# Attention heads of a two-layer trunk: one value product per head with features on partitions, probabilities scaled before they are turned, turned two blocks behind, and a rotation of one operation

## What is computed

```python
q = (_rms_norm(cq, g_q) @ w_uq).reshape(b, s, MLA_HEADS, QK_NOPE + QK_ROPE)      # 8 heads, 64 + 32
kv = (_rms_norm(ckv, g_kv) @ w_ukv).reshape(b, s, MLA_HEADS, QK_NOPE + V_DIM)    # 64 + 64
q_pe = _rope(q_pe, cos[:, :, None], sin[:, :, None])
k_pe = _rope(k_pe, cos, sin)
for i in range(s // Q_BLOCK):                                                     # 4 blocks of 128 queries
    scores = (q_nope . k_nope + q_pe . k_pe) * ATTN_SCALE, causal, over (i + 1) * 128 keys
    probs = jax.nn.softmax(scores, axis=-1)
    outs.append(jnp.einsum('bhqk,bkhd->bqhd', probs, v[:, :k_end]))
y = jnp.concatenate([pool_mixer, spatial_gating, attention], axis=-1)
return y @ w_out
```

## Time and profile before

| | us |
|---|---|
| median of 3 runs (2265.99 to 2271.66) | 2271.29 |
| the profiled execution | 2274.56 |
| its span | 2272.8 |
| mean granted PE clock over the span (share of full) | 0.898 |
| PE busy | 1938.4 (85%) |
| DVE busy | 1248.5 (55%) |
| ACT busy | 913.2 (40%) |

### The profile page before, as it was taken

The page is one execution under the profiler, slowest core; times in us unless marked ns, Lnnn a source line. Parts: engine busy times, 40 slices in busy tenths (PEclk is TensorE's granted clock), DMA queues, the critical chain, the costliest instruction groups (busy, mean ns, idle before and its releaser), DMA issues. The chain is left out here.

```text
span 2272.8 us, 31364 instructions
## 1 busy us (share of the span) xinstructions
PE 1938.4 (85%) x8992; PEld 1339.1 (59%) x8993; DVE 1248.5 (55%) x1918; ACT 913.2 (40%) x1339; POOL 364.6 (16%) x281
## 2 busy tenths in 40 slices
PE   6888889889999998999378888988899999999960
PEld 3655577666666665665165456757666666666640
DVE  2457636546464554643754774557464555546437
ACT  2323421435453544543132442146454545444531
POOL 0100300112221211211020030012122221111210
PEclk9888889989998999999689888999899999999985
DMA  6135224589999999998733622457799999999956
GB/s 247 68 126 185 74 105 167 212 334 389 399 376 374 352 385 333 385 374 327 287 102 99 207 79 78 192 187 293 301 400 399 361 373 371 380 363 375 352 220 272
DMA packets 128818, 619.42 MB, mean 273 GB/s; under 512 B 22530, under 2 KB 25602, under 8 KB 73490
## 3 DMA queue, kind: packets, MB, share of 16 engines
q1 hardware_dynamic: 105876, 550.62, 63.5%
q0 software_dynamic: 22784, 67.13, 8.3%
HBM read 584.13 MB, written 46.14 MB: 277 GB/s over the span
## 5 line engine op out<-in xcount | busy, mean ns | idle before, releaser
L1564 DVE TENSOR_TENSOR w_lod_r<-raw_d,w_hid_r 128x2048 fp32r<-128x2048 f32 x72 | 165.5, 2298 | 270.2 <-ACT w_hid_r L1337 270.2
L1262 POOL DMA_INDIRECT mixT<-h_rows,gidx x104 | 144.8, 1392 | 793.6 <-issue 599.1
L1757 PE MATMUL bank<-mod,hbT 128*64 128x512 f32 x512 | 226.6, 595 | 0.0
L1757 PE MATMUL bank<-hT,hbT 128*64 128x512 f32 x512 | 226.6, 595 | 0.0
L1276 POOL DMA_INDIRECT y_rows<-mixT,sidx x104 | 143.8, 1383 | 460.2 <-issue 360.6
L1352 ACT ACTIVATE mixT<-bank 128x512 f32<-128x512 f32 x208 | 113.0, 599 | 211.4 <-PE bank L1776 116.9
L1723 PEld LDWEIGHTS bank<-meta,mod 128*128 128x128 f32 x1088 | 141.3, 201 | 69.0 <-issue 65.2
L1561 DVE TENSOR_TENSOR w_loa_r<-raw_gu,w_hia_r 128x2048 fp32r<-128x2048 f32 x72 | 164.8, 2289 | 18.2 <-ACT w_hia_r L1334 18.1
L1723 PE MATMUL bank<-meta,mod 128*128 x1088 | 140.6, 256 | 30.8 <-DVE mod L1540 30.7
L1561 DVE TENSOR_TENSOR w_lob_r<-raw_gu,w_hib_r 128x2048 fp32r<-128x2048 f32 x72 | 164.3, 2282 | 0.0
L1377 ACT ACTIVATE mod<-bank 128x256 f32<-128x256 f32 x104 | 39.7, 382 | 307.1 <-PE bank L1736 175.5
(11 more groups left out here) (362 smaller groups left out, 4140.0 us busy)
## 6 DMA issues: line engine op xcount, KB each, us to landing
raw_d<-in_w_down SPq DMA_DIRECT2D x104, 1024.0 KB, 11.0
raw_gu<-in_w_gate SPq DMA_DIRECT2D x72, 1024.0 KB, 9.4
raw_gu<-in_w_up SPq DMA_DIRECT2D x72, 1024.0 KB, 16.3
w_ada_sb<-in_w_ada SPq DMA_DIRECT2D x32, 1024.0 KB, 5.2
hT<-in_w_gate SPq DMA_DIRECT2D x32, 1024.0 KB, 7.9
hT<-in_w_up SPq DMA_DIRECT2D x32, 1024.0 KB, 13.8
mod<-in_w_gate SPq DMA_DIRECT2D x32, 1024.0 KB, 12.8
mod<-in_w_up SPq DMA_DIRECT2D x32, 1024.0 KB, 17.9
```

Source lines behind the costliest of these rows:

```text
L1262: by_rows(s, lambda rows: pool.indirect_dma_start(out=hb[s.par][0:rows], out_offset=None, in_=h2_dram, in_offset=bass.IndirectOffsetOnAxis ...
L1564: dve.tensor_tensor(w_lo[2][:], raw_d[s.down_at][:], w_hi[2][:].bitcast(F32), ALU.subtract).then_inc(lo[2], 1)
L1757: i = pe.matmul(bank_g[s.par][lane, :], hbT[:, c, lane], pair_gu[k][:, :, c, :], start=c == 0, stop=c == DC - 1)
```

## The change

In the head loop and behind it:

- `attend` is done once for a head, not once for a block: values stationary (64 columns), turned probabilities moving, four products of 512, 384, 256 and 128 columns into lane 0 to 63 (even head) or 64 to 127 (odd head) of bank 6. The result has features on partitions, as `mixed_out` wants it. `probsT` holds a whole head, in one buffer.
- The division comes ahead of the turning: DVE takes the reciprocal of each block's row sum (`share` on DVE), ACT multiplies `probs` by it in place (`share` on ACT). `probs` has four buffers, not two.
- PE turns block n-2 in iteration n, projects on i = 0, and attends to the head before on i = 2. ACT does `head_out` on i = 1. DVE rotates on i = 2 and spreads its multiply-adds as 3, 2, 0, 3.
- `rotate` is one product of 64 partitions: queries and their turned copy, times cos and sin (sin is copied behind cos once, at the start). The sum is left to the score product, whose contraction grows from 96 to 128 rows; the common key part is therefore written twice per buffer (four sums, not two).
- The transposes L938, L729 and the copies of them go. ACT copies bank 6 out once for two heads. `w_out_hi` is made in heads 5 and 6, four parts in each; `mod_out(11)` comes last.

```diff
-        q_sb, k_sb = qk[0:QK, 0:2, :], qk[0:QK, 2:4, :]
+        q_sb, k_sb = qk[:, 0:2, :], qk[:, 2:4, :]
-        o_att = hT[:, 4:8, :]
-        probs = h[:, :, 0:512]
-        probsT = h[:, :, 512:1024]
+        probs = h[:].rearrange("p a (b n) -> p (a b) n", b=2)
+        probsT = hT[:, 4:8, :]
...
                     hd, i = n // TJ, n % TJ
                     act.wait_ge(s_PT, n + 1)
-                    if n >= 2:
-                        act.wait_ge(s_O, n - 1)
-                    act.activation(probsT[:, n % 2, 0:(i + 1) * P], bank[5][:, 0:(i + 1) * P], ACT.Copy).then_inc(s_PTe, 1)
-                    if i == 0 and hd >= 1:
-                        o_out(hd - 1)
+                    wait(act, s_O, hd)
+                    act.activation(probsT[:, 0:i + 1, i * P:i * P + P], bank[5][:, 0:(i + 1) * P].rearrange("p (k q) -> p k q", q=P), ACT.Copy).then_inc(s_PTe, 1)
+
+                def o_out(m):
+
+                    act.wait_ge(s_O, 2 * m + 2)
+                    act.activation(mixT[:, 4 + m, :], bank[6][:], ACT.Copy).then_inc(s_oe, 1)
...
+                def exponent(n):
+
+                    act.wait_ge(s_max, n + 1)
+                    wait(act, s_PT, n - 3)
+                    act.activation(probs[:, n % 4, 0:(n % TJ + 1) * P], bank[3 + n % 2][:, 0:(n % TJ + 1) * P], ACT.Exp,
+                                   scale=SCALE, bias=rs[:, N_SOFT + n:N_SOFT + n + 1],
+                                   accum_out=rs[:, 2 * N_SOFT + n:2 * N_SOFT + n + 1]).then_inc(s_exp, 1)
+
+                def share(n):
+
+                    row = probs[:, n % 4, 0:(n % TJ + 1) * P]
+                    act.wait_ge(s_rec, n + 1)
+                    act.mul(row, row, rs[:, 3 * N_SOFT + n:3 * N_SOFT + n + 1]).then_inc(s_prob, 1)
...
+                for n in range(N_SOFT + 2):
+                    hd, i = n // TJ, n % TJ
+                    if n < N_SOFT:
+                        exponent(n)
+                    if 1 <= n <= N_SOFT:
+                        share(n - 1)
+                    if i == 1 and hd + 1 < HEADS:
+                        head_out(hd + 1)
+                    if n >= 2:
+                        pt(n - 2)
+                    if n in (11, 19, 27):
+                        o_out((n - 11) // 8)
...
                 for b in range(2):
-                    i = dve.tensor_tensor(k_sb[R, b, :], k_pe[R, 0, :], k_pe[R, 1, :], ALU.add)
+                    for to in (R, ROT):
+                        i = dve.tensor_tensor(k_sb[to, b, :], k_pe[R, 0, :], k_pe[R, 1, :], ALU.add)
...
-                    dve.wait_ge(s_qn, hd + 1)
-                    link(dve.tensor_tensor(tmp[R, 0, :], bank[hd % 2][R, :], cos[R, :], ALU.mult))
-                    link(dve.tensor_tensor(tmp[R, 1, :], bank[hd % 2][ROT, :], sin[ROT, :], ALU.mult))
-                    dve.tensor_tensor(q_sb[R, hd % 2, :], tmp[R, 0, :], tmp[R, 1, :], ALU.add).then_inc(s_q, 1)
+                    both = slice(NOPE, P)
+                    dve.tensor_tensor(q_sb[both, hd % 2, :], bank[hd % 2][both, :], cos[both, :], ALU.mult).then_inc(s_q, 1)
...
+                def share(n):
+
+                    dve.wait_ge(s_exp, n + 1)
+                    dve.reciprocal(rs[:, 3 * N_SOFT + n:3 * N_SOFT + n + 1], rs[:, 2 * N_SOFT + n:2 * N_SOFT + n + 1]).then_inc(s_rec, 1)
...
-                        if i == 3 and hd + 1 < HEADS:
+                        if n >= 1:
+                            share(n - 1)
+                        if i == 2 and hd + 1 < HEADS:
                             rotate(hd + 1)
-                        ada(4 + hd, (range(0, 3), range(3, 5), range(5, 8), ())[i])
+                        ada(4 + hd, (range(0, 3), range(3, 5), (), range(5, 8))[i])
...
                 def turn(n):
                     i = n % TJ
-                    pe.wait_ge(s_exp, n + 1)
+                    pe.wait_ge(s_prob, n + 1)
                     wait(pe, s_PTe, n)
...
+                def attend(hd):
+
+                    pe.wait_ge(s_PTe, (hd + 1) * TJ)
+                    wait(pe, s_oe, hd // 2)
+                    lane = slice(VDIM * (hd % 2), VDIM * (hd % 2) + VDIM)
+                    for k in range(TJ):
+                        ins_ = pe.matmul(bank[6][lane, k * P:], v_att[:, k, hd, :], probsT[:, k, k * P:], start=k == 0, stop=k == TJ - 1)
                     ins_.then_inc(s_O, 1)
...
-                for n in range(N_SOFT):
+                for n in range(N_SOFT + 2):
                     if n + 1 < N_SOFT:
                         scores(n + 1)
-                    turn(n)
-                    if n % TJ == 1 and n // TJ + 1 < HEADS:
+                    if n < N_SOFT and n % TJ == 0 and n // TJ + 1 < HEADS:
                         project(n // TJ + 1)
-                    if n % TJ == 2 and n >= TJ:
+                    if n >= 2:
+                        turn(n - 2)
+                        if n % TJ == 2 and n > TJ:
+                            attend(n // TJ - 1)
+                    if n < N_SOFT and n % TJ == 2 and n >= TJ:
                         ada(3 + n // TJ)
-                    if n >= 1:
-                        attend(n - 1)
-                attend(N_SOFT - 1)
+                attend(HEADS - 1)
```

More of the change, by code:

```diff
@@ L283, in _ @@
                 act.wait_ge(s_start, 32 + 4 + 16)
+                act.activation(cos[QK:P, :], sin[QK:P, :], ACT.Copy).then_inc(s_start, 1)
+                act.wait_ge(s_start, 32 + 4 + 17)
                 first_out(act, s_first).then_inc(s_cond, 1)
@@ L465, in _, with weight_lo @@
                 i.then_inc(s_rot, 1)
-                for n in range(2 * DC):
+                def weight_lo(n):
                     b, m = n // DC, n % DC
@@ L470, in _ @@
                     pool.tensor_tensor(w_out_lo[:, m, 512 * b:512 * b + 512], part, w_out_hi[b][m].bitcast(F32), ALU.subtract).then_inc(s_w_lo, 1)
+                for n in range(2 * DC):
+                    weight_lo(n)
             @block.scalar
@@ L575, in _ @@
+                act.wait_ge(s_oe, 3)
+                act.wait_ge(s_S, N_SOFT)
+                for m in range(3):
+                    act.activation(mix_hi[1][:, m, :], mixT[:, 4 + m, :], ACT.Copy).then_inc(s_mix_hi, 1)
+                act.wait_ge(s_O, HEADS)
+                act.activation(mix_hi[1][:, 3, :], bank[6][:], ACT.Copy).then_inc(s_mix_hi, 1)
                 for m in range(DC):
                     weight_hi(1, m)
-                for i in range(TJ):
-                    act.wait_ge(s_oT, i + 1)
-                    act.activation(mix_hi[1][:, :, i * P:i * P + P], bank[(5, 7)[i % 2]][:].rearrange("p (m t) -> p m t", m=4), ACT.Copy).then_inc(s_mix_hi, 1)
+                mod_out(11)
@@ L721, in _ @@
                         n += 1
+                share(N_SOFT - 1)
                 mixed_lo(TJ - 1)
-                dve.wait_ge(s_exp, N_SOFT)
-                link(dve.reciprocal(rs[:, 3 * N_SOFT:4 * N_SOFT], rs[:, 2 * N_SOFT:3 * N_SOFT]))
-                dve.wait_ge(s_oe, HEADS)
-                sums = rs[:, 3 * N_SOFT:4 * N_SOFT].rearrange("p (h i) -> p h i", i=TJ)
-                for i in range(TJ):
-                    dst = o_att[:, i, :].rearrange("p (h d) -> p h d", d=VDIM)
-                    dve.tensor_tensor(dst, dst, sums[:, :, i].unsqueeze(2).to_broadcast([P, HEADS, VDIM]), ALU.mult).then_inc(s_o, 1)
-                for i in range(TJ):
-                    dve.wait_ge(s_mix_hi, 5 + i)
-                    dve.tensor_tensor(mix_lo[:, 4:8, i * P:i * P + P], bank[(5, 7)[i % 2]][:].rearrange("p (m t) -> p m t", m=4),
-                                      mix_hi[1][:, :, i * P:i * P + P].bitcast(F32), ALU.subtract).then_inc(s_mix_lo, 1)
+                for m in range(4, 7):
+                    mixed_lo(m)
+                dve.wait_ge(s_mix_hi, 8)
+                dve.tensor_tensor(mix_lo[:, 7, :], bank[6][:], mix_hi[1][:, 3, :].bitcast(F32), ALU.subtract).then_inc(s_mix_lo, 1)
                 dve.wait_ge(s_mod, 2)
```

62 lines of the change are left out of this document (11 added, 51 removed).

## The result

| | before | after |
|---|---|---|
| median of the runs, us | 2269.42 (4 runs, 2265.99 to 2271.66) | 2234.52 (4 runs, 2228.35 to 2237.35) |
| profiled execution, us | 2274.56 | 2237.35 |
| its span, us | 2272.8 | 2235.6 |
| mean granted clock over the span | 0.898 | 0.912 |

The ratio is 0.9844, 95% interval 0.9824 to 0.9863: faster by 1.6%, 35 us. Forecast was 2232, range 2210 to 2256.

What follows compares the result with a forecast made beforehand. Head period taken as DVE chain, rotation hole and clock penalty. Loops and drain -36.1, transposes -6.2, key sums +2.6 made -39.7 us from the profiled 2274.56: 2234.9, stated as 2232 because that execution lay 3.3 above the median; range 2210 to 2256.

Steps and rivals of the forecast that it cites:

- the forecast case: Head loop: periods of 10.9 to 12.3 us a head, whole time 2221 to 2245 us; chance 0.55.
- The rotation hole and the clock: Head loop: PE's 2.8 us hole a head closes, the clock falls less often, mean clock 0.87 or more.
- DVE 10.2 us a head: DVE in the head loop: 10.4, minus 1.4 for rotation, plus 0.6 for reciprocals, plus 0.5 between operations.
- The weight units: Condition's multiply-adds in the loop: later fetch makes an 11.1 us cycle; DVE idles 0.5 to 1 us in each second block.
- rival A: Whole kernel: everything hidden, landing 4.4 us, clock stays up, period 10.4, drain 8.5, time 2212; chance 0.17.
- Value product the same on PE: Attend on PE: 2.1 us a head before, 2.15 after at full clock, nothing gained or lost.
- PE's slack: PE in the head loop: 9.1 us of work a head at full clock, about 2 us idle in pieces.
- Drain 10.5 us: Behind the last head's last maximum, up to mixed_out: 6.1 us before, 8.5 to 12 after, taken as 10.5.
- Transposes, minus 3.1 a layer: Behind the head loop: PE's transposes go, saving 3.1 us, twice 6.2, with their substitutes hidden under mixed_out.
- Key sums, plus 1.3 a layer: Ahead of the head loop: two more sums on DVE's path cost 1.3 us, twice 2.6.
- No wait of PE's loads for the rotation: Head loop, sign to see in the profile after: PE's loads, which waited 17.2 us for L702, no longer wait.

Runs made afterwards that it cites:

- e1: Kernel before, with only the three-operation rotation moved to the end of block i = 2 on DVE; 2275.1 us, ratio 1.0020.
- e5: Changed kernel, with the one-operation rotation back on block i = 3 behind the maximum and multiply-adds spread 3, 2, 3, 0; 2231.4 us, ratio 0.9830.
- e2: Kernel before, with the one-operation rotation in the old place, its four key sums and 128 contraction rows; 2240.2 us, ratio 0.9870.
- e8: Changed kernel, with the old three-operation rotation (two key sums, 96 rows) in the new place; 2252.9 us, ratio 0.9935.
- e3: Changed kernel, with multiply-adds spread 3, 2, 3, 0, so the last three come one block earlier; 2234.9 us, ratio 0.9858.
- e9: Changed kernel with multiply-adds 3, 2, 3, 0, key sums in DVE's idle stretch, and half of mixed_out ahead of the last value product; 2222.8 us, ratio 0.9785.
- e6: Changed kernel, with each head's four value products issued twice; 2261.7 us, ratio 0.9966.
- e4: Changed kernel, with the four key sums moved into DVE's idle stretch ahead of the gating product; 2228.3 us, ratio 0.9823.

## Why the prediction was right, and where its reasons were not

The time and the forecast case were right (period 11.5 forecast; 11.9 and 11.8 measured over six heads). Point by point:

- **The rotation hole and the clock.** Right that the head's period was a DVE chain, a hole and a clock penalty, and that the clock would recover (0.87 or more forecast, 0.95 and 0.94 measured). PE's own hole was overstated: of the 2.8 us between L700 and the next maximum it idles 1.62. Nor does the clock fall after every such gap: behind the one at 223.05 it stays at 1.00. Wrong in the step "the rotation on i = 2 is done a whole block before scores of the next head need it: the hole closes". The place did nothing where it was tried: e1 moves the hole onto the exponential, e5 puts it back without loss. The one operation alone (e2) gives 28 us, everything else alone (e8) 16. The sum priced that operation at 1.4 us of DVE a head; with the clock that stays up it was worth 3.2 in e2.
- **DVE 10.2 us a head.** A little high. The head of 10.91 us above has 9.26 us busy, 1.20 of waiting for weights and 0.45 of gaps, so 9.7. The reciprocal lasts 0.15 us, as L715 does, but the next operation starts 0.07 us behind its start (214.22, 214.29): four cost 0.3 us, not 0.6.
- **The weight units.** Right in kind and place (k = 4 of the second block), mis-sized in the first layer: 0.5 to 1 us a head forecast, 12.2 us in six of eight heads measured, 1.1 to 3.4 us each. In the second layer it is 7.1 us in all, 0.9 a head. The landing time was taken as 5.2 us. The median over the loop after is 6.2 us in the first layer and 5.2 in the second; before it is 5.2 over the whole first loop, with the same rows of `w_out` in it, so why it is longer there stays open. A landing of 4.4 us, on which rival A stands, shows in no run: the shortest of all is 4.9. And the wait was worth less than it shows (e3).
- **Value product the same on PE.** Right: eight records take 234.53 to 236.83, 2.3 us in e9, 2.15 forecast. By the Trainium skill's isolated gap ("TensorE: Matmul & The Clock Gate", Back-to-back issue gap), an estimate of 0.5 us for the narrow ones, the wide product would have been a loss; the trace at 252.86 does not agree with it. The load time on the same page of the Trainium skill (LDWEIGHTS), columns over 1.2 GHz, 107 ns for 128 columns, agrees with the 0.105 us measured at full clock. At half clock the same records stand 0.20 us apart (eight from 211.53 to 213.13), which it does not give.
- **PE's slack.** "PE still idles about 2 us a head" was nearly right for the head above (10.91 less 8.77 busy), and most of it can be used: of 2.15 us added a head e6 shows 0.6 to 0.7 between the rotations. Over the two layers 54% of what e6 adds shows in the stretches, most of it behind the last rotation, and about three quarters in the medians.
- **Drain 10.5 us.** Right on the first layer (10.7), short in the other three drains of the two profiles (12.8, 12.6, 12.5). It costs the change 4.5 and 8.6 us against before, 5 and 8 against e2 (5.5 and 4.6). With the weight waits that is why the whole change has the longer loop than e2.
- **Transposes, minus 3.1 a layer.** From `mixed_out` to the last gate product it is 49.4 and 48.3 us before, 45.0 after: 4.4 and 3.3. The first has 1.2 us of half clock in it (0.69 over its first 4 us) that was not in my term.
- **Key sums, plus 1.3 a layer.** A little small. From the second key product to the query copy it takes 17.2 us before with two sums, 18.7 and 19.4 after with four, 15.9 in e4 with none: the two of the change cost 1.5 and 2.2 us.
- **No wait of PE's loads for the rotation.** Not met: 4.8 and 3.4 us a loop are left.

In sum, the loops gave 17.1 + 12.5 us where 36.1 was forecast, and what lies behind them gave 7.7 where 6.2 was. The key sums took 3.7 where 2.6 was forecast. That is 33.6 us less where the sum said 39.7. The profile shows 37.2 less: the other 3.6 lie in the start (1.7 more) and in the experts (2.3 and 3.0 less), which the forecast left alone. So a part of how near the time came is luck.

## What to carry to other kernels

Price a part of a change by itself before crediting it, and the rest without it: here one algebraic step (let the product's contraction do the sum) gave 28 us alone, all the other edits 16 alone, and both 33 to 35. Moving a late operation ahead of the operation that feeds a queue one block behind only moved the hole (e1); shortening it paid (e2). A longer lag may help too, but was not run alone. When a consumer of a double-buffered transfer is moved later, check the cycle issue, landing, first use, last use, with the landing time of the busiest stretch.

## What was not expected of the hardware

Idle pieces of PE that differ by less than a microsecond go with a different clock over a whole loop: with waits of 1.62 and 1.65 us once a head (before, e1) the first loop runs at 0.78, with 0.82 us (e2) at 0.93, with as many columns of PE's work. That makes 1.4 us of DVE worth 3.2 us of period. And the same experts, up to the second key product, take from 892 to 901 us behind first mixers that differ by a few microseconds; nothing here shows why.
